# Reordering the way from the first layer's experts to the gated convolution

## The reference, cut to what matters

```python
# end of layer 0: x = x + g_f * ec_moe(...)        (the scattered sum over experts)
hx = modulate(x, norm_mix[1], sh_m, sc_m)           # rmsnorm over the features, times (1+scale), plus shift

def short_conv_mixer(h, w_in, conv_w, w_out):
    b_gate, c_gate, val = jnp.split(h @ w_in, 3, axis=-1)     # w_in: 1024 x 3072
    u = c_gate * val
    y = conv3(u)                                              # three taps along the tokens, per feature
    return (b_gate * y) @ w_out
```

## Time and profile before

| | us |
|---|---|
| median of three runs | 1577.53 |
| lowest, highest | 1577.27, 1578.59 |
| the profiled execution: its own time | 1578.1 |
| the profiled execution: span from first to last instruction | 1576.3 |
| TensorE busy in it | 1473.2 (93%) |
| VectorE, ScalarE, GpSimd busy | 666.7, 230.6, 79.6 |

### The profile page before, as it was taken

The page is one execution under the profiler, slowest core; times in us unless marked ns, Lnnn a source line. Parts: engine busy times, 40 slices in busy tenths (PEclk is TensorE's granted clock), DMA queues, the critical chain, the costliest instruction groups (busy, mean ns, idle before and its releaser), DMA issues.

```text
span 1576.3 us, 16119 instructions
## 1 busy us (share of the span) xinstructions
PE 1473.2 (93%) x6738; PEld 687.9 (44%) x6738; DVE 666.7 (42%) x1139; ACT 230.6 (15%) x416; POOL 79.6 (5%) x72
## 2 busy tenths in 40 slices
PE   7999999999799999998989899999899999988987
PEld 4555655554333333333323688854333333322332
DVE  2578877434622322323222778735423232321223
ACT  2134345223200000000000200014000000000000
POOL 0010010000000000000000032000100000000000
PEclk9999999999899999999999999999999999999999
DMA  9962310696499999999999912453799999999996
GB/s 322 378 210 86 107 68 40 253 388 240 168 416 425 426 427 428 425 428 427 426 428 424 368 54 107 180 214 110 288 426 427 427 428 426 426 426 428 427 427 286
DMA packets 68593, 504.96 MB, mean 320 GB/s; under 512 B 8127, under 2 KB 18590, under 8 KB 39850
## 3 DMA queue, kind: packets, MB, share of 16 engines
q1 hardware_dynamic: 64618, 490.83, 76.3%
q0 software_dynamic: 2752, 8.92, 1.5%
q10 hardware_dynamic: 1152, 4.19, 0.7%
HBM read 497.62 MB, written 6.29 MB: 320 GB/s over the span
## 4 chain that ended last, share of the span: by engine, by line
PE 72%; DMA 19%; DVE 6%; ACT 2%; issue 1%; SPq 1%; DVEq 0%; ACTq 0%; POOLq 0%
PE ps L1114 31%; DMA work<-in_exp_w_up_dram 11%; PE ps L1198 9%; PE ps L965 7%; DMA ring<-in_exp_w_up_dram 6%; PE ps L1130 5%; PE ps L872 3%; PE ps L831 2%; PE ps L663 2%; PE ps L776 2%; PE ps L772 2%; PE ps L835 1%; PE ps L858 1%; PE ps L1152 1%; DMA ring<-in_ada_w_dram 1%; PE ps L1098 1%
## 5 line engine op out<-in xcount | busy, mean ns | idle before, releaser
L1114 PE MATMUL ps<-ring,work 128*64 128x512 f32 x1824 | 407.1, 595 | 31.6 <-ACT work L1479 13.0
L1114 PE MATMUL ps<-work 128*64 128x512 f32 x1248 | 279.7, 595 | 21.4 <-ACT work L1479 8.9
L2067 DVE TENSOR_TENSOR work<-ps,work 128x1024 f32<-128x1024 f32 x120 | 141.3, 1219 | 283.9 <-PE ps L1130 283.9
L1114 PEld LDWEIGHTS ps<-ring,work 128*64 128x64 f32 x1824 | 127.1, 137 | 292.9 <-issue 248.7
L1114 PEld LDWEIGHTS ps<-work 128*64 128x64 f32 x1248 | 87.0, 137 | 200.1 <-issue 169.8
L1130 PE MATMUL ps<-work 64*128 64x512 f32 x480 | 119.2, 615 | 0.0
L2085 DVE SCALAR_TENSOR_TENSOR work<-ps,gate_e,gate_ffn 128x512 f32<-128x512 f32 x32 | 24.0, 751 | 185.8 <-PE ps L1114 185.8
L2078 DVE TENSOR_TENSOR work<-work,ps 128x512 f32<-128x512 f32 x32 | 22.0, 687 | 170.4 <-issue 152.2
L1475 ACT ACTIVATE work<-ps 128x512 f32<-128x512 f32 x32 | 19.1, 597 | 482.4 <-PE ps L1114 482.4
L2255 POOL DMA_INDIRECT work<-xn_rows,row_no x32 | 30.7, 958 | 1033.4 <-PE ps L1098 730.5
L1479 ACT ACTIVATE work<-ps 128x512 f32<-128x512 f32 x32 | 19.1, 597 | 372.8 <-PE ps L1152 372.8
(11 more groups left out here) (324 smaller groups left out, 1395.5 us busy)
## 6 DMA issues: line engine op xcount, KB each, us to landing
ring<-in_exp_w_gate_dram SPq DMA_DIRECT2D x38, 2048.0 KB, 31.4
ring<-in_exp_w_up_dram SPq DMA_DIRECT2D x37, 2048.0 KB, 32.9
ring<-in_exp_w_down_dram SPq DMA_DIRECT2D x37, 2048.0 KB, 35.3
work<-in_exp_w_up_dram SPq DMA_DIRECT2D x27, 2048.0 KB, 30.9
work<-in_exp_w_gate_dram SPq DMA_DIRECT2D x24, 2048.0 KB, 35.8
work<-in_exp_w_down_dram SPq DMA_DIRECT2D x23, 2048.0 KB, 38.5
ring<-in_ada_w_dram SPq DMA_DIRECT2D x34, 1024.0 KB, 7.7
ring<-in_ada_w_dram SPq DMA_DIRECT2D x4, 2048.0 KB, 7.7
```

What stands on the lines that cost most here:

```text
L1114: last = mm(PS[64 * h:64 * h + 64, bank, :], lhsT[:, m * P + 64 * j:m * P + 64 * j + 64], slot_rows[sl][:, m, h * BANK:(h + 1) * BANK], st ...
L2067: v.tensor_tensor(row, PS[:, b:b + 2, :], row, ALU.add).then_inc(added[L], 1)
```

## The change

Five things, in five lists of instructions.

1. VectorE adds only tiles 0 and 1, normalizes both, then adds tile 2, takes half 0, adds tile 3, and normalizes 2 and 3.
2. ScalarE takes its part of half 0 after the squares of tile 2 and before those of tile 3.
3. TensorE does P1 of triple 1 right behind P1 of triple 0, both ahead of the transposes of tiles 2 and 3; P2 of triple 0 stands between those two transposes, P2 of triple 1 behind them.
4. The weight sums of triple 0 leave VectorE and are done by GpSimd after `experts(0)`, in four instructions, three of which wait for their own end before the next is issued. They start when slot 6 is loaded and slot 4's last chunk has been used.
5. P6 of triple 0 waits for GpSimd's new semaphore; the counts of `w_summed` drop by one.

```diff
             first_product(0)
+            first_product(1)
             for t in (2, 3):
                 pe.wait_ge(xn_in, NT + t + 1)
                 conv_T(t)
-            first_product(1)
-            pe.wait_ge(inT_a, KC)
-            conv_product(0, "P2")
-            conv_product(1, "P2")
+                pe.wait_ge(inT_a, KC)
+                conv_product(t - 2, "P2")
             for u in range(TRIPLES):
                 if u >= 2:
                     first_product(u)
-                pe.wait_ge(w_summed, u + 1)
+                if u == 0:
+                    pe.wait_ge(first_sums, 1)
+                else:
+                    pe.wait_ge(w_summed, u)
...
+            for t in range(XT - 1):
+                squares(t)
+            take_conv(0)
+            squares(XT - 1)
+            take_conv(1)
...
-            for t in range(XT - 1):
+            for t in range(2):
                 add_last(0, t)
-            normalize(0)
-            normalize(1)
-            add_last(0, XT - 1)
+            for t in range(2):
+                normalize(t)
+            add_last(0, 2)
+            take_conv(0)
+            add_last(0, 3)
             normalize(2)
-            take_conv(0)
-            normalize(XT - 1)
-            weight_sums(0)
+            normalize(3)
             take_conv(1)
             row_sums()
...
             experts(0)
+            sl = CONV_SLOT[PART[0], 0]
+            A11, A12, A21, A22 = halves_of(0)
+            S1, S2, S4 = w_sums[0]
+            pool.wait_ge(used[0], last_use(SUMS_SLOT) + 1)
+            pool.wait_ge(slot_in[sl], 16 * conv_loads(sl))
+            own.link(g.tensor_tensor(S1, A21, A22, ALU.add))
+            own.link(g.tensor_tensor(A21, A11, A21, ALU.subtract))
+            own.link(g.tensor_tensor(S2, S1, A11, ALU.subtract))
+            g.tensor_tensor(S4, A12, S2, ALU.subtract).then_inc(first_sums, 1)
```

More of the change, by code:

```diff
@@ L291, in build @@
         h_summed, w_summed, z_ready, x_final = (sem(n) for n in ("h_summed", "w_summed", "z_ready", "x_final"))
+        first_sums = sem("first_sums")
         out_stored, w_scaled = sem("out_stored"), sem("w_scaled")
@@ L1484, in _, with squares @@
             f(stat[:, 95:96], eps, ACT.Sqrt)
-            for t in range(XT):
+            def squares(t):
                 act.wait_ge(added[0], XT * (E - 1) + t + 1)
@@ L1488, in _, with take_conv @@
                 f(stat[:, 8 + t:9 + t], stat[:, t:t + 1], ACT.Sqrt, bias=eps, scale=1.0 / D).then_inc(x_final, 1)
-            for half in range(2):
+            def take_conv(half):
                 for g in range(KC // 2, KC):
```

## The result

| | median us | range | runs |
|---|---|---|---|
| before | 1578.54 | 1576.09 to 1580.90 | 22 |
| changed | 1580.69 | 1578.37 to 1584.01 | 22 |

The ratio is 1.0016, 95% interval 1.0010 to 1.0022: the changed kernel is 2.5 us slower (1.6 to 3.5), by less than the 0.2% up to which I called it no change, though the interval leaves no change out. The kernel before came out 1.0 higher here than in its first three runs, so the forecast of +1.4 on its time is to be compared with +2.5.

The account below looks back on a forecast made before the run. TensorE, busy nearly everywhere, was taken as the bound, the start of its steady run setting the time. Half 0 0.3 earlier, the way to P6 0.35 longer and a 1.3 clock fall gave +1.4, 1578.9 us; range 1576.2 to 1581.1.

Parts of the forecast that it names:

- T2 takes TensorE's place as what P6 waits for: Ahead of P6 of triple 0: tile 3's later transposes delay T2, P6 starts 12.05 us after half 0, TensorE waits 2.3.
- Blocking between GpSimd and the multiplies: Normalizing tiles 0 and 1: VectorE's multiplies wait for whole GpSimd instructions, tile 1 ready at 881.5 in place of 880.7.
- Half 0 is taken earlier: Start of taking half 0: 882.65 in place of 882.93, 0.3 us earlier; 881.85 without blocking.
- ScalarE's new order and VectorE's free 2.7 us hide: Ahead of half 1: tile 3 normalized at 888.6, before its transposes at 889.8; 2.7 us freed on VectorE gain nothing.
- The clock: TensorE around half 0: idle time about unchanged, so one fall to 1.2 GHz is expected again, costing 1.3 us.
- Rival B: New 2.3 us wait ahead of P6: clock falls a second time, another 1.7 us, +3.1 or 1580.6; chance 0.22.
- Rival A: Ahead of half 0: GpSimd's sums miss the multiplies and the clock holds, -0.7 us or 1576.8; chance 0.17.
- C: Same stretch: GpSimd blocks the multiplies but the clock doesn't fall, +0.1 us or 1577.6; chance 0.16.

Follow-up runs that it names:

- e1: Kernel before with only TensorE's new order (P1 of triple 1 ahead of the transposes of tiles 2 and 3, P2 of triple 0 between): ratio 1.0032, +5.0 us.
- e4: Changed kernel with P1 of triple 1 still ahead of the transposes of tiles 2 and 3, but both P2 behind them: ratio 1.0002 to the kernel before.
- e2: Kernel before with only triple 0's weight sums moved to GpSimd: ratio 0.9999 to the kernel before.
- e12: Changed kernel with triple 0's weight sums back on VectorE, between the last normalize and half 1: ratio 1.0022 to the kernel before.
- e3: Changed kernel with TensorE's old order put back: ratio 1.0002 to the kernel before.
- e6: Kernel before with TensorE's new order alone plus four idle matmuls in the wait ahead of P6 of triple 0: ratio 1.0019 to the kernel before.
- e11: Changed kernel with GpSimd's four sums started only when tiles 0 and 1 are normalized: ratio 1.0012 to the kernel before.

## Why the prediction was right

*T2 takes TensorE's place as what P6 waits for.* Right, and the step that carried the forecast. 12.05 from half 0 to P6 was forecast; it was 12.31 (885.68 to 897.99), with a wait of 2.29 where 2.3 was said. e1 and e4 show that the order of the products alone makes the wait.

*Blocking between GpSimd and the multiplies.* Right in kind, too large in size: 0.8 forecast, 0.34 measured. VectorE's and GpSimd's timelines of the changed kernel:

```profile
882.17 0.78 DVE L2110 TENSOR_SCALAR work<-work,stat 128x1024 f32<-128x1024 f32 x1
...
883.53 1.09 DVE L2110 TENSOR_SCALAR work<-work,stat 128x1024 f32<-128x1024 f32 x1
```

```profile
881.12 1.27 POOL L2290 TENSOR_TENSOR ring<-ring 128x512 f32<-128x512 f32 x1
882.47 1.60 POOL L2291 TENSOR_TENSOR ada_part<-ring 128x512 f32<-128x512 f32 x1
```

The third instruction ends at 882.39 and the first multiply at 882.95; the fourth ends at 884.07 and the second multiply at 884.62; in e2 it is 0.55 again. A blocked multiply ends 0.55 after GpSimd's instruction, not 0.75, as if 0.2 of it ran while it was blocked, and GpSimd's own instruction loses 0.33, not 0.5 to 0.7. I had counted both at full length. That the adds out of PSUM are free beside GpSimd holds: 1.21 to 1.22 as alone. This bears out the Trainium skill, SBUF — State Buffer, section Who interferes with whom, on 128x1024 too, but for "fully blocks", from which 0.2 us of the multiply are an exception here.

*Half 0 is taken earlier.* By 0.83 (7.71 after `y_s`, before 8.54), not by 0.3, mostly for the reason above. The rest of the way ate it: 12.31 against 11.7 with the slow clock in it.

*ScalarE's new order and VectorE's free 2.7 us hide.* Right in this kernel: tile 3 is normalized at 891.43 and wanted at 892.94, and e12 shows VectorE's time to be worth 0.3, through the row sums. It hides only because TensorE's new order wants tile 3 late; with the old order (e3) TensorE waits for it.

*The clock.* This term was not borne out, and luck has a part in how near the sum came. I took TensorE's idle time ahead of half 0 to be about what it was and put one fall of 1.3 us there as most likely (0.38). The idle time went from 2.9 (1.05 and 1.89) to 1.9 (0.26, 0.59 and 1.03), and the changed kernel's profile has no fall in the stretch. The other side of the sum was off too: I set the single profile of before, which had fallen, equal to the kernel's usual run, while e1, e2 and e6 have the same hole without a fall. The two errors point opposite ways: 1.3 too much on the changed kernel, 1.7 of slow clock that I left in the kernel before. At full clock on both sides my own working gives 894.7 against 892.9 for P6, +1.8; measured are +1.6 of way. So the schedule carried the forecast, and the +1.4 was near for a reason that it doesn't name. The +0.9 between the way and the measured +2.5 is inside the interval (1.6 to 3.5) and may be clock.

*Rival B* (a second fall, in the new wait, 1580.6) has the number, 1580.69, but not the mechanism, as far as one profile tells: the clock is 1.00 behind the changed kernel's wait. Only e12, with a wait of 2.92, has the fall there. *Rival A* (it does what it says) fell with the wait. *C* (blocking, no fall) is what the changed profile shows: +0.1 was forecast for it against the profile of before, and P5 of triple 1 and the end of the convolution came out level with that profile. Against a kernel before with its clock up, C's schedule costs the 1.6.

## What to carry to other kernels

Work that is pulled into a hole delays what stands behind it in the same engine's list: before moving it, follow the longest chain that starts behind it (here transpose, take, two sums) to the next instruction of that engine, and move only as much as keeps that chain's end ahead. Parts of a change that hide behind each other must be measured together as well as alone: here 2.4 and 1.2 of way make 1.6. When a single profile has a slow clock in the stretch, work out the full-clock time before comparing, and look through the whole span for the other falls before putting a difference of spans, or of mean clocks, down to the stretch.

## What was not expected of the hardware

The fall of 3.4 us at 1.2 GHz doesn't follow from the hole alone: with 1.88 or 1.89 idle us ahead of P1 and 1.05 to 1.61 a little ahead, one of four profiles has it (before, not e1, e2 or e6); behind 2.29 idle us none of three has (changed, e1, e11), and behind 2.92 the one there is has (e12). Four idle matmuls of 1.7 us together, off the way, went with a mean granted clock 0.0014 to 0.0016 higher and medians 2.1 and 3.2 us lower, though on other chips and with overlapping intervals. An instruction of VectorE that is blocked by GpSimd's ended 0.55 us after it, 0.2 less than its own length of 0.75 (the changed kernel and e2). A sum of VectorE with both inputs in SBUF took 1.64 in place of 0.69 beside GpSimd, and by that lengthened TensorE's way by 0.95 in e12.
